# Reading cached values, retention states and delta states in half as many TensorE insertions

## The reference

```python
def decoder_layer(x, pos, mem_k, mem_v, s_ret, s_gdn, conv_buf, p):
    h = x + 0.5 * rms_norm(swiglu(rms_norm(x, ...), ...), ...)
    m, s_ret, s_gdn, conv_buf = token_mixing(rms_norm(h, ...), ...)
    h = h + rms_norm(m, ...)
    h = h + 0.5 * rms_norm(swiglu(rms_norm(h, ...), ...), ...)
    return h, s_ret, s_gdn, conv_buf

# token_mixing, for one sample and one head
prob = softmax(q @ mem_k.T / 16); o_mem = prob @ mem_v        # mem_v: 256 x 256, cached
S = gamma * S + outer(k, v);      o_ret = q @ S               # S: 128 x 256, state_ret
S = e^g * (I - beta k k^T) S + beta * outer(k, v); o_gdn = q @ S   # S: 128 x 256, state_gdn
```

## Time and profile before

| | |
|---|---|
| median of 3 runs | 1933.48 us (1932.43 to 1934.76) |
| profiled execution | 1930.05 us |
| its span | 1928.3 us |
| TensorE matmul, busy | 1849.2 us (96%) |
| VectorE, busy | 1349.1 us (70%) |
| ScalarE, busy | 903.6 us (47%) |
| mean DMA rate | 193 GB/s |
| granted TensorE clock, mean | 0.99 |

### The profile page before, as it was taken

How to read it: one execution, slowest core, us unless ns; L and a number is a source line. 1 busy time by engine, 2 the same in 40 slices (tenths; PEclk the granted TensorE clock), 3 DMA queues, 4 the chain that set the end, 5 groups by cost and what they waited for, 6 DMA issues and landing times. The chain is left out here.

```text
span 1928.3 us, 40625 instructions
## 1 busy us (share of the span) xinstructions
PE 1849.2 (96%) x16354; PEld 1785.9 (93%) x16354; DVE 1349.1 (70%) x2070; ACT 903.6 (47%) x1048; POOL 120.2 (6%) x176
## 2 busy tenths in 40 slices
PE   6999999999998999999999999999999899999997
PEld 6999999988888999999999999998888899999997
DVE  5777577758666867776577756777676776877755
ACT  3533355456654264533354334464566435353433
POOL 0000001101210100000000000110111010000000
PEclk9999999999999999999999999999999999999998
DMA  7676657666764556565667766665666564556653
GB/s 234 187 204 193 182 178 230 213 218 211 253 208 155 180 177 206 164 183 160 182 196 215 200 177 187 214 227 196 232 232 208 166 194 158 175 187 186 185 163 113
DMA packets 436075, 372.48 MB, mean 193 GB/s; under 512 B 9474, under 2 KB 413316, under 8 KB 435010
## 3 DMA queue, kind: packets, MB, share of 16 engines
q1 hardware_dynamic: 411728, 278.76, 48.5%
q0 software_dynamic: 24160, 91.12, 13.6%
HBM read 343.16 MB, written 26.69 MB: 192 GB/s over the span
## 5 line engine op out<-in xcount | busy, mean ns | idle before, releaser
L1715 DVE TENSOR_TENSOR wl<-raw,wh 128x2048 fp32r<-128x2048 f32 (+1 forms) x282 | 603.7, 2141 | 192.3 <-ACT wh L1261 165.5
L1261 ACT CAST wh<-raw 128x2048 fp32r<-128x2048 f32 (+1 forms) x282 | 503.9, 1787 | 250.2 <-PE proj L652 121.7
L652 PE MATMUL proj<-xl,wh 128*128 128x264 f32 x2624 | 380.8, 286 | 0.5 <-DVEq L1846 0.5
L652 PE MATMUL proj<-xh,wh 128*128 128x264 f32 x2624 | 380.7, 288 | 0.0
L652 PE MATMUL proj<-xh,wl 128*128 128x264 f32 x2624 | 371.1, 284 | 2.1 <-DVE wl L1715 2.1
L652 PEld LDWEIGHTS proj<-xl,wh 128*128 128x128 f32 x2624 | 342.0, 189 | 14.1 <-issue 13.2
L652 PEld LDWEIGHTS proj<-xh,wh 128*128 128x128 f32 x2624 | 341.2, 189 | 1.9
L652 PEld LDWEIGHTS proj<-xh,wl 128*128 128x128 f32 x2624 | 339.1, 188 | 3.4 <-DVE wl L1715 3.4
L671 PE MATMUL proj<-hl,wh 128*128 128x264 f32 x704 | 173.3, 283 | 0.0
L670 PE MATMUL proj<-hh,wh 128*128 128x264 f32 x704 | 173.0, 283 | 0.0
L1282 ACT ACTIVATE gate<-gate 128x264 f32<-128x264 f32 x88 | 37.4, 425 | 248.0 <-DVEq L1747 248.0
(11 more groups left out here) (444 smaller groups left out, 2383.0 us busy)
## 6 DMA issues: line engine op xcount, KB each, us to landing
raw<-ffn_w_in SPq DMA_DIRECT2D x176, 512.0 KB, 5.1
raw<-w_in SPq DMA_DIRECT2D x80, 1024.0 KB, 5.6
raw<-ffn_w_out SPq DMA_DIRECT2D x64, 704.0 KB, 4.6
sring<-cache_mem_k POOLq DMA_DIRECT2D x32, 512.0 KB, 5.0
sring<-cache_mem_v POOLq DMA_DIRECT2D x32, 512.0 KB, 4.4
out<-sring POOLq DMA_DIRECT2D x32, 512.0 KB, 4.3
sring<-state_gdn POOLq DMA_DIRECT2D x32, 512.0 KB, 5.4
raw<-w_mem_v SPq DMA_DIRECT2D x10, 1024.0 KB, 6.3
```

What stands on the lines that cost most here:

```text
L652: mm = pe.matmul(o, w[:, s, k * 256 + t * P:k * 256 + (t + 1) * P], a[:, k, :], **go)
L1261: act.copy(wh[:, slot, 0:size], raw[:, slot, 0:size]).then_inc(hi_done[slot], 1)
L1715: dve.tensor_sub(wl[:, slot, 0:size], raw[:, slot, 0:size], wh[:, slot, 0:size].bitcast(F32)).then_inc(split_done[slot], 1)
```

## The change

The steps sv, rd and gd are merged in pairs. sv{g // 2} now stands in the odd groups of gq and reads four units (two samples) into the two halves of one bank. rd{g // 2} stands in the even groups of x2 and reads two units into one bank. gd{g // 2} stands in groups 1 and 3 of rg and reads four units into two banks. VectorE adds the parts of all of them behind one wait. The samples of odd number in x2 are therefore read one group earlier than before; the first samples' values and delta states are read one group later. In `STEPS` the steps are listed accordingly, and with that the banks of the steps around them change. Loads, stores, matmuls and accumulations stay the same in number.

```diff
-            for x in (mid, f"sv{g}", last) if x]
+            for x in (mid, f"sv{g // 2}" if g % 2 else None, last) if x]
...
-            for x in (f"rd{g}",) + ((f"rS{g - 1}",) if g else ("svt",)) + more]
-         + ["gkn", "gd0", "rn0", "rn1", "gd1", "gbr0", "gG0", "gQ0", "gd2", "gbr1", "gG1", "gQ1", "gd3", "gT"]
+            for x in (() if g % 2 else (f"rd{g // 2}",)) + ((f"rS{g - 1}",) if g else ("svt",)) + more]
+         + ["gkn", "rn0", "rn1", "gd0", "gbr0", "gG0", "gQ0", "gbr1", "gG1", "gQ1", "gd1", "gT"]
...
                 def values(g, t, k):
-                    if (t, k) != (1, 3):
+                    if (g % 2, t, k) != (1, 1, 3):
                         return
...
-                    o = begin(l, f"sv{g}")
-                    for half in range(2):
-                        slot = unit_wait(pe, l, V_UNIT + 2 * g + half)
-                        mm = four_heads(o[:, 0, 0:DV], lambda h: pv[:, half, :], slot, start=(half == 0), stop=(half == 1))
-                        if half:
-                            end(mm, f"sv{g}")
+                    o = begin(l, f"sv{g // 2}")
+                    for n in range(4):
+                        half = n % 2
+                        slot = unit_wait(pe, l, V_UNIT + 2 * (g - 1) + n)
+                        mm = four_heads(o[:, 0, n // 2 * DV:(n // 2 + 1) * DV], lambda h: pv[:, half, :], slot,
+                                        start=(half == 0), stop=(half == 1))
+                        if n == 3:
+                            end(mm, f"sv{g // 2}")
                         else:
                             mm.then_inc(unit_used[slot], 1)
...
                 def read_retention(g, t, k):
-                    if (t, k) == (0, 3):
-                        o = begin(l, f"rd{g}")
-                        slot = unit_wait(pe, l, R_UNIT + g)
-                        end(four_heads(o[:, 0, 0:DV], lambda h: rqw[:, h, :], slot, start=True, stop=True), f"rd{g}")
+                    if (g % 2, t, k) == (0, 0, 3):
+                        o = begin(l, f"rd{g // 2}")
+                        for c in range(2):
+                            slot = unit_wait(pe, l, R_UNIT + g + c)
+                            mm = four_heads(o[:, 0, c * DV:(c + 1) * DV], lambda h: rqw[:, h, :], slot, start=True, stop=True)
+                        end(mm, f"rd{g // 2}")
...
                 def read_delta(g, t, k):
-                    if (t, k) != (1, 3):
+                    if (g % 2, t, k) != (1, 1, 3):
                         return
-                    o = begin(l, f"gd{g}")
-                    for c in range(2):
-                        slot = unit_wait(pe, l, D_UNIT + 2 * g + c)
+                    o = begin(l, f"gd{g // 2}")
+                    for c in range(4):
+                        slot = unit_wait(pe, l, D_UNIT + 2 * (g - 1) + c)
...
                 def values(g):
+                    if g % 2 == 0:
+                        return
+                    o = take(dve, l, f"sv{g // 2}")[:, 0, :]
+                    for b in (g - 1, g):
+                        own_part(accv, o[:, (b % 2) * DV:(b % 2 + 1) * DV], own_val, b)
+                    release(dve, f"sv{g // 2}")
+                    dve.sem_inc(unit_used[(V_UNIT + 2 * g + 1) % SRING], 1)
...
                 def update_retention(g):
-                    if g < NS:
-                        own_part(accr, take(dve, l, f"rd{g}")[:, 0, 0:DV], own_row, g)
-                        release(dve, f"rd{g}")
+                    if g < NS and g % 2 == 0:
+                        o = take(dve, l, f"rd{g // 2}")[:, 0, :]
+                        for c in range(2):
+                            own_part(accr, o[:, c * DV:(c + 1) * DV], own_row, g + c)
+                        release(dve, f"rd{g // 2}")
...
                 def read_delta(k):
+                    if k % 2 == 0:
+                        return
+                    o = flat(f"gd{k // 2}")
+                    for b in range(2 * k - 2, 2 * k + 2):
+                        own_part(accd, o[:, (b % 4) * DV:(b % 4 + 1) * DV], own_row, b)
+                    release(dve, f"gd{k // 2}")
+                    for b in range(2 * k - 2, 2 * k + 2):
                         dve.sem_inc(unit_used[(D_UNIT + b) % SRING], 1)
```

More of the change, by code:

```diff
@@ L100 @@
 ONE_BANK = ("n1 n2 n3 p1 p2 p3 gaw gab smt spt rks gcs rqd gcol gev gqd gkS gmt svt rdt gdt gT gw0 gw1 mqs0 mqs1 mqs2 mqs3 "
-            + " ".join(f"{n}{k}" for n in ("sp", "rd", "gd", "sv") for k in range(2 * NS)) + " "
+            + " ".join(f"{n}{k}" for n in ("sp", "rd", "sv") for k in range(2 * NS)) + " "
             + " ".join(f"{n}{s}" for n in ("gG", "gQ") + tuple(f"{n}{g}" for n in ("gy", "gt") for g in range(LEVELS)) for s in range(2)) + " " + " ".join(f"{n}{g}" for n in ("gc", "gu") for g in range(SMALL))).split()
@@ L883, in values @@
                 def values(g, t, k):
-                    if (t, k) != (1, 3):
+                    if (g % 2, t, k) != (1, 1, 3):
                         return
-                    if g == 0:
+                    if g == 1:
                         ready("sptd")
-                    o = begin(l, f"sv{g}")
-                    for half in range(2):
-                        slot = unit_wait(pe, l, V_UNIT + 2 * g + half)
-                        mm = four_heads(o[:, 0, 0:DV], lambda h: pv[:, half, :], slot, start=(half == 0), stop=(half == 1))
-                        if half:
-                            end(mm, f"sv{g}")
+                    o = begin(l, f"sv{g // 2}")
[6 more added lines that the diff above has]
+                            end(mm, f"sv{g // 2}")
                         else:
@@ L1017, in read_delta @@
                 def read_delta(g, t, k):
-                    if (t, k) != (1, 3):
+                    if (g % 2, t, k) != (1, 1, 3):
                         return
-                    o = begin(l, f"gd{g}")
-                    for c in range(2):
-                        slot = unit_wait(pe, l, D_UNIT + 2 * g + c)
-                        mm = four_heads(o[:, 0, c * DV:(c + 1) * DV], lambda h: gqw[:, h, :], slot, start=True, stop=True)
-                    end(mm, f"gd{g}")
+                    o = begin(l, f"gd{g // 2}")
+                    for c in range(4):
+                        slot = unit_wait(pe, l, D_UNIT + 2 * (g - 1) + c)
+                        mm = four_heads(o[:, c // 2, (c % 2) * DV:(c % 2 + 1) * DV], lambda h: gqw[:, h, :], slot, start=True, stop=True)
+                    end(mm, f"gd{g // 2}")
                 def blocks(o, left, right):
@@ L2099, in own_part, with values @@
                         order(ts_(total[:], o, rows[:, 0:1], None, ALU.mult))
[L2101 to L2105, removed]
+                def values(g):
+                    if g % 2 == 0:
[5 more added lines that the diff above has]
+                    dve.sem_inc(unit_used[(V_UNIT + 2 * g + 1) % SRING], 1)
                 def retention_middle(g):
```

## The result

The changed kernel took **1939.76 us** (median of 20 runs, 1930.85 to 1947.89); the kernel before, run beside it, 1930.90 (20 runs). The ratio is 1.0045, 95% interval 1.0034 to 1.0056: slower by about 9 us.

A forecast was written before the change was run, and what follows sets the result against it. TensorE, busy 96% of the span, was taken as the bound. Terms -0.6 (first x2), -0.7 (first rg), -1.6 (second x2), -0.35 (second rg) gave -3.2; clock +0.8 made -2.4 of 1933.48: 1931.1 us, range 1926.0 to 1937.5.

The forecast's parts named there:

- Visits and banks, gq: First layer's gq: fewer visits and bank waits put TensorE 3.1 us earlier, of which VectorE's pace leaves -2.8 us.
- the four bank waits of the earlier trace: TensorE's waits for banks in gq, x2 and rg, 3.63 us a layer, were to lose their cause.
- The R1 hole: First layer, rd0 in x2: R1, freed late, lands at 456.3, so TensorE idles 2.1 us.
- the net of -2.9 at group 2: First layer's x2: with visit rd1 and the bank wait of gct0 gone too, TensorE is 2.9 us earlier.
- The fall at 463.8: First layer's x2: the existing clock fall, costing 1.7 us, moves to the hole for R1, at no change.
- R5 is late too (about 1 us) but R7's chain does not start from it, so adds nothing.: x2: R5 comes about 1 us late, but the load of R7 does not depend on it, so no cost.
- R7: 2.8 us idle.: First layer, rd3 in x2: R7 lands at 509.1, wanted at 506.3; the 2.8 us idle leaves x2 at -0.6.
- D3 limit stays in layer 2: Second layer's rg: TensorE already idles 2.24 us for D3; that end stays, so only -0.34 us is gained.
- rg at -0.7: First layer's rg: -0.34 us by gbr0, another -0.34 from VectorE's accumulations around decays(1) and gT; -0.7 in all.
- half a fall: Clock term: the new hole for R7 in x2 may bring one more clock fall; counted as half, +0.8 us.
- slower by the clock: Rival, chance 0.15: holes at rd0 and rd3 halve the clock, two more falls per layer; +5.2 us, 1938.7.
- The range: Whole kernel: 1926.0 to 1937.5 us, leaving out the ends of the first two rivals.

The follow-up runs named there:

- sv_only: Against the kernel before, only the values' reads (sv) are merged, rd and gd stay as before; ratio 0.9978, measured again 0.9977.
- wait_early: The kernel before, nothing merged; TensorE only waits ahead of the reads of R0, R2, R4, R6 for the next unit too; ratio 1.0049.
- rd_only: Against the kernel before, only the retention reads (rd) are merged, sv and gd stay as before; ratio 1.0073 to before.
- rd_first: The changed kernel, but R4 to R7 are read one by one as before; median 1927.17 us, ratio 0.9987 to before.
- odd_gd_late: The changed kernel with rd in x2's odd groups and the second four delta parts added behind the copy of gT; ratio 0.9988 to before.
- rd_odd: The changed kernel with the merged retention reads moved to x2's odd groups, so no unit is read early; ratio 1.0004 to before.
- odd_no_gd: The changed kernel with the merged retention reads in x2's odd groups and the delta reads as before; ratio 0.9984 to before.
- no_store: The changed kernel without the stores of the samples' retention states (write-back left out); median 1925.31 us, ratio 0.9964 to before.

## Why the prediction was wrong, point by point

**Visits and banks, gq.** Right. gq was to end 2.8 us earlier; it did by 2.2 to 2.4, and sv_only keeps 3.6 us up to the end of the first layer's x2. Of the four bank waits of the earlier trace rows none is left.

**The R1 hole.** Right in place and size (2.1 us, measured 2.10), in the clock fall behind it, and in the net of -2.9 at group 2 (-2.8). The fall at 463.8 did move. The match to the tenth is in part luck: a wait of 0.52 us for R0, which the prediction did not have, and a landing of 6.3 us in place of 6.1 nearly cancel.

**"R5 is late too (about 1 us) but R7's chain does not start from it, so adds nothing."** This is the step that failed, in both halves. R5 was issued 2.55 us earlier than before, as worked out, but took 8.2 us to land against 4.9, the longest of R5's landings in any profile here, and the hole was 3.9 us. With 4.9 it would have been about 0.5, an estimate from these rows; in the second layer, with 5.4, it was 1.61. And it adds far from nothing. A stretch of halved clock follows, and R7's chain does start from it: the prediction took VectorE's updates to run some 2.5 us early whatever TensorE waited for, but the update of R3 needs rS3, which stands behind rd2 in TensorE's order, and it came 6.1 us late. That such waits are lost in full is shown by wait_early: 7.1 us at full clock and 3.2 of clock, with nothing merged.

**"R7: 2.8 us idle."** No such hole. R7 landed 4.5 us after its issue, not 7.8, and TensorE came 4 to 5 us later than assumed, because of R5. rd_only has it (2.9 us, with a landing of 7.9). By its own terms the prediction should have had TensorE 3.5 us early there and not 3.0 (two units more and two visits less lie between: 0.9 - 1.6), which would have changed the idle time and not the end.

**"D3 limit stays in layer 2", none in layer 1.** The first half is right (2.42 us, against 2.24 before). The second is wrong: 3.5 us. The prediction had no hole there because it gave the store of R7 and the load of D3 no landing times of their own; they took 7.5 and 6.5 us, against 5.0 and 5.1 before. Without the merge of R4 to R7 (rd_first) there is no hole in either layer, and in the first D3 lands at 536.5 in place of 546.9; but odd_gd_late has the hole too. So R5 does not explain it, and what sets it, most likely the moment of the weight load, was not tried.

**rg at -0.7.** The terms (1.34 us less before decays(1), 1.00 more before gT) were set against each other as if both lay on one path. The 1.00 before gT lies wholly ahead of gc0, whose wait went from 0.85 to 2.2 us; gd alone measured -1.5 us at full clock and +3.4 by the clock, a loss of 2 us (3 by its ratio).

**The clock.** The forecast gave it half a fall, +0.8 us. It was +7.0. The rival "slower by the clock" had 1938.7, with four falls more at 1.7 (6.8 us) at rd0 and rd3; result and size are near it, in part by luck: the falls stand behind rd0, rd2, and the waits of rg, x0 and the output phases, and in x2, where this rival has its sign, there is one more than before. Its chance of 0.15 was too low: half of the evidence used against it was the single 2.24 us hole without a fall. In the profiles 14 of the 19 waits for a state of 1.9 us or more have a fall in them or within 1.6 us behind them; of the six longest (3.05 to 5.31 us) it is four, of the others ten. The Trainium skill ("TensorE: Matmul & The Clock Gate", Why this matters for your kernels) warns of drops behind idle gaps between bursts of matmuls; most of these waits agree, though most are shorter than the gaps that the page speaks of. By whole kernels the tie is loose: those with a wait of 1.9 us or more for a state in the first layer lost 2.0 to 8.1 us more to the clock than before did, those with none -0.2 to +6.2 (rd_odd the most). So T3, falls that have nothing to do with holes, is not ruled out for a part of the 7.0 us.

**The range.** Its upper end lies near the second rival's time; nothing in it stood for a long landing of R5 or for D3 in the first layer. The base flattered the forecast: 1933.48, from three runs, is 2.6 us above the 1930.90 that the kernel before took beside the changed one, so that in absolute time the miss is 8.7 us and against before it is more. The miss of 11.2 us (-2.4 forecast, +8.8 by the means) has two terms: 5.0 at full clock (-3.2 forecast, +1.8 measured), from R5, D3 and gc0, and 6.2 of clock (+0.8 against +7.0).

## What to carry to other kernels

Before an insertion is merged with a later one, list for each unit it reads when it lands, and which engines wait for the merged step or for what stands behind it in their own order. Of several waits, follow the one that ends last: here VectorE's update waited for rS3 and not for the merged read itself. Give every store and load its own landing time, with the spread that the trace shows: R5's single landing took 3.3 us longer than in the profile before. Merge toward the later group, or merge only reads whose data has long been there, and allow for a clock fall behind most new waits of 2 us.

## What was not expected of the hardware

**Whether the clock falls at a hole depends on more than that hole.** The output phases of the first layer are the same in both kernels, with the same waits. Before:

```profile
739.81 0.39 PE L652 MATMUL proj<-mh,wh 128*128 128x264 f32 x1 [1.30 <-DVEq L1846]
741.77 0.39 PE L652 MATMUL proj<-mh,wh 128*128 128x264 f32 x1 [1.57 <-DVEq L1846]
```

After:

```profile
743.88 0.39 PE L652 MATMUL proj<-mh,wh 128*128 128x264 f32 x1 [1.23 <-DVEq L1850]
745.83 0.39 PE L652 MATMUL proj<-mh,wh 128*128 128x264 f32 x1 [1.57 <-DVEq L1850]
```

The windows behind them, of before and of after:

```profile
742.00:748.00 6.00, 6.00 (x51) 6.00 (x51) 3.73 (x5) 1.20 (x3) 0.00 (x0) 1.00 0.50 172
```

```profile
746.60:750.00 3.40, 3.40 (x17) 3.40 (x17) 1.91 (x3) 0.40 (x1) 0.00 (x0) 0.50 0.22 61
```

The same pair of holes is followed by 2.4 GHz in one profile and by 1.2 GHz in the other. So runs of one kernel differ (1930.85 us at a mean clock of 0.992, 1947.89 at 0.982), and one profiled run does not price a hole; a mean over runs does.

**A landing of 512 KB is not one number.** Among R0 to R7 of the first layer it took between 4.0 us (R6 of rd_only) and 10.7 (R2 of odd_no_gd), with R5 at 4.9 before and 8.2 after. R5's load is issued behind a 1 MB weight load in all but one kernel: 1.70 us behind it before and 0.94 in the changed one; in no_store, where no weight load is in flight with it, it took 4.3 and 4.4 us. Of R0 to R2, which the merged values issue together, each lands later than the one ahead (4.2, 6.3 and 8.6 us in the changed kernel).

**Open.** rd_odd and odd_no_gd lose 2 to 6 us to the clock without a hole for a state; their falls were not traced to a cause. Whether a weight load issued together with a store slows it, and so makes D3's hole, was not tried.
